# Page slots that rotate, and pooling tables that are loaded earlier, in a one-core decoder step

## The reference

```
Layer 0 mixer, samples (mla_sample): for each of the 8 sequences
    rows   = cache[16 pages] (2048 x 320), and the new row
    kn     = rmsnorm(latent @ w_uk) per head;  s = (qn.kn + qr.kr) * scale
    p      = softmax(s);  ctx = p @ latent;  o = ctx @ w_uv
Layer 1 mixer (pool_mixer): per group of 256 channels
    d      = mean over the last 2/4/8/16 positions - the position itself
    y      = (d @ w_pool[group]) * pool_scale
Both layers (peer): q = x @ w_q; s = q @ subkeys; two top-16, top-16 of their sums
    e      = 128 experts per token;  g = softmax(best)
    y      = sum_k g_k * gelu(x . u[e_k]) * v[e_k]
Every sub-layer: rmsnorm, (1 + scale) * h + shift from c, gated residual add
```

## Time and profile before

| | |
|---|---|
| Time of the runs | 3461.2 us (3457.77 to 3462.1) |
| Span of the profiled execution | 3450.9 us, from first to last instruction |
| Time beside the span | 10.3 us (3461.2 - 3450.9) |
| PE, DVE, ACT, POOL busy | 80%, 66%, 30%, 35% of the span |
| Moved from HBM | 1258.79 MB |
| Chain that ended last | PE 44%, DMA 27%, DVE 15% |

### The profile page before, as it was taken

The page is one execution under the profiler, slowest core; times in us unless marked ns, Lnnn a source line. Parts: engine busy times, 40 slices in busy tenths (PEclk is TensorE's granted clock), DMA queues, the critical chain, the costliest instruction groups (busy, mean ns, idle before and its releaser), DMA issues.

```text
span 3450.9 us, 39502 instructions
## 1 busy us (share of the span) xinstructions
PE 2764.3 (80%) x11255; PEld 1233.7 (36%) x11255; DVE 2273.6 (66%) x6378; ACT 1043.5 (30%) x4438; POOL 1212.1 (35%) x1077
## 2 busy tenths in 40 slices
PE   7889889879989858988989779889875675566765
PEld 2355544434434323434433234334331231112321
DVE  2544668887787856768777566777866545565455
ACT  1222324424434413434434314434411111111111
POOL 0000024333333424434434334433344444543343
PEclk9989999989999979999999989999888876777777
DMA  8740079999999989999999999999999999999998
GB/s 326 285 176 34 14 275 406 401 374 397 366 395 407 396 332 401 413 390 417 413 401 412 396 357 412 415 404 410 395 396 414 418 421 408 421 389 376 421 417 356
DMA packets 201396, 1264.74 MB, mean 366 GB/s; under 512 B 23689, under 2 KB 44730, under 8 KB 61393
## 3 DMA queue, kind: packets, MB, share of 16 engines
q0 software_dynamic: 150784, 1091.03, 77.5%
q1 hardware_dynamic: 50393, 171.18, 12.9%
HBM read 1258.79 MB, written 3.79 MB: 366 GB/s over the span
## 4 chain that ended last, share of the span: by engine, by line
PE 44%; DMA 27%; DVE 15%; issue 7%; ACT 3%; POOL 2%; SPq 2%; DVEq 0%; POOLq 0%; ACTq 0%; PEldq 0%
PE bank L1146 15%; DMA ring<-in_uv,work 10%; PE bank L884 7%; DMA mod_mix<-in_uv,work 7%; DMA big<-in_uv,work 6%; PE bank L996 6%; DVE ring L2028 2%; PE bank L901 2%; DMA ring<-in_w_ada 2%; PE bank L830 2%; ACT work L1475 1%; PE bank L698 1%; PE bank L728 1%; PE bank L636 1%; PE bank L872 1%
## 5 line engine op out<-in xcount | busy, mean ns | idle before, releaser
L1146 PE MATMUL bank<-ring,work 128*64 128x512 f32 (+1 forms) x2080 | 903.6, 709 | 272.3 <-ACT work L1475 272.2
L1514 POOL DMA_INDIRECT ring<-in_uv,work x520 | 602.8, 1159 | 937.9 <-PE bank L1146 810.0
L2028 DVE CUSTOM_DVE_ANT_0 ring<-ring,mod_smp 128x1024 f32<-128x1024 f32 x512 | 621.8, 1224 | 264.7 <-DMA ring<-in_uv,work 257.7
L1463 ACT ACTIVATE work<-work 128x2 f32<-128x2 f32 x520 | 105.1, 202 | 1485.7 <-DVE work L2028 1485.2
L1514 POOL DMA_INDIRECT big<-in_uv,work x260 | 305.1, 1174 | 663.3 <-PE bank L1146 361.2
L884 PE MATMUL bank<-big 128*128 128x512 f32 x1024 | 515.2, 626 | 0.0
L1146 PEld LDWEIGHTS bank<-ring,work 128*64 128x64 f32 (+1 forms) x2080 | 209.3, 153 | 623.5 <-ACT work L1475 386.2
L1146 PE MATMUL bank<-big,work 128*64 128x512 f32 (+1 forms) x1040 | 308.0, 710 | 153.1 <-ACT work L1475 153.1
L2028 DVE CUSTOM_DVE_ANT_0 big<-big,mod_smp 128x1024 f32<-128x1024 f32 x256 | 309.5, 1224 | 133.4 <-DMA big<-in_uv,work 129.7
L1146 PE MATMUL bank<-work 128*64 128x512 f32 (+1 forms) x520 | 295.6, 697 | 106.2 <-ACT work L1475 106.1
L1475 ACT ACTIVATE work<-small,work 128x64 f32<-128x64 f32 (+1 forms) x1040 | 303.2, 339 | 144.7 <-DVE work L2038 138.8
(11 more groups left out here) (301 smaller groups left out, 3419.2 us busy)
## 6 DMA issues: line engine op xcount, KB each, us to landing
big<-in_wk SPq DMA_DIRECT2D x48, 1152.0 KB, 10.5
ring<-in_w_ada SPq DMA_DIRECT2D x64, 768.0 KB
work<-in_cache_mla SPq DMA_DIRECT2D x104, 160.0 KB, 6.5
ring<-in_uv,work POOLq DMA_INDIRECT x520, 12.0
big<-in_uv,work POOLq DMA_INDIRECT x260, 11.3
ring<-in_w_mla_out SPq DMA_DIRECT2D x1, 4096.0 KB, 14.0
big<-in_w_mla_out SPq DMA_DIRECT2D x4, 1024.0 KB, 11.5
mod_smp<-in_cache_mla SPq DMA_DIRECT2D x24, 160.0 KB, 11.1
```

Of the source, the lines that this page charges most:

```text
L1146: last = mm(out, diag[:, t % 2, j, 0:min(m, HALF)], s[:, D + half * 512:D + (half + 1) * 512], start=(k == 0 and (n < S0 or j == 0)), stop ...
L1463: act.activation(acts[:, t % 2 * GRP:(t % 2 + 1) * GRP], dots[:, t % 2 * GRP:(t % 2 + 1) * GRP], ACT.Gelu)\
L1514: pool.indirect_dma_start(slot[g % SLOTS], None, T["uv"].rearrange("l e d -> (l e) d"), bass.IndirectOffsetOnAxis(index[:, k * GRP + j:k * ...
L2028: dve.tensor_tensor_reduce(u, u, hb, 1.0, 0.0, ALU.mult, ALU.add, dots[:, at:at + 1]).then_inc(sem("dots_set"), 1)
```

## The change

Sample pages get 25 slots instead of 16. Page g of sequence r lies in slot (16 r + g) mod 25, nine of which are in a new buffer `pages_ahead` of 12 KB to a partition; the scratch for POOL's transfer descriptors is set to 4096 bytes to a partition. SP loads the next sequence's first 9 pages at `tail - 8` and its other 7 and the own row at `tail + 5`. Its first page is computed at `tail + 2` instead of `tail + 7`; `project_page` now waits for the step of the softmax before it whose part of PSUM bank 6 it writes, and `spread_max` writes to columns 256 to 383 instead of 0 to 127. The last sequence's `tail` is turn 314 instead of 345; `out_turn`, 360, and the number of turns stay as they were.

For the pooling mixer, two modulation rows, `norm_mix`, band and w_pool are loaded at turn -11. `norm_mix` goes to a free `hid` buffer. The third row and `pool_scale` are loaded at turn -1.

```diff
-        PGRP = 4
+        PGRP, EARLY = 4, 9
+        pages_ahead = sb("pages_ahead", [P, 3 * D])
...
-        cached = [cached_all[:, g * ROW:(g + 1) * ROW] for g in range(13)]
-        cached += [mod_smp[:, 2, g * ROW:(g + 1) * ROW] for g in range(3)]
+        page_slots = [cached_all[:, g * ROW:(g + 1) * ROW] for g in range(13)]
+        page_slots += [mod_smp[:, 2, g * ROW:(g + 1) * ROW] for g in range(3)]
+        page_slots += [pages_ahead[:, g * ROW:(g + 1) * ROW] for g in range(EARLY)]
+        cached = lambda r, g: page_slots[(r * NPG + g) % len(page_slots)]
...
             tail[r_] = t_
-            t_ += 7
+            t_ += 2
...
-                    if t == tail[r - 1] + 4:
+                    if t == tail[r - 1] - 8:
+                        if r >= 2:
+                            sp.wait_ge(sem("ctx_ps"), r - 1)
+                        sp.wait_ge(sem("page_ps"), (r - 1) * NPG + EARLY)
+                        load_pages(r, 0, EARLY)
+                    if t == tail[r - 1] + 5:
                         sp.wait_ge(sem("ctx_ps"), r)
-                        load_pages(r)
+                        load_pages(r, EARLY, NPG)
...
-                    if t == mix_at[n] - 2:
+                    if t == mix_at[n] - 11:
+                        sp.wait_ge(sem("qT_ps"), n // 2 * PH)
+                        for m, k in ((0, 1), (1, 0)):
+                            ld(mod_pool[:, m, :], ada_rows[1, NC - 1, k * D:(k + 1) * D].partition_broadcast(P), "mods_in")
+                        ld(hid[n % 4], T["norm_mix"][1].partition_broadcast(P), "mods_in")
+                        sp.wait_ge(sem("sco_ps"), n // 2 * PH)
+                        pooling_weights()
+                    if t == mix_at[n] - 1:
                         sp.wait_ge(sem("choice_set"), n // 2 * 2 * PH)
-                        mods(mod_pool, 1, 0, "prompt", P, T["norm_mix"][1], gain_pool)
+                        ld(mod_pool[:, 2, :], ada_rows[1, NC - 1, 2 * D:3 * D].partition_broadcast(P), "pool_gain_in")
+                        ld(gain_pool, T["pool_scale"][0].partition_broadcast(P), "pool_gain_in")
                     if t == mix_at[n] + 2:
                         w.next("mods_set")
-                        ld(gain_pool, T["pool_scale"][0].partition_broadcast(P), "pool_gain_in")
...
-                for n in mix_at:
-                    if t == mix_at[n] - 2:
-                        sp.wait_ge(sem("sco_ps"), n // 2 * PH)
-                        pooling_weights()
...
-                if g == 0 and r:
-                    pe.wait_ge(sem("ctx_ready"), r)
+                if r:
+                    gone = page_at[r, g] - tail[r - 1]
+                    if gone >= 7:
+                        pe.wait_ge(sem("ctx_ready"), r)
+                    elif gone >= 5:
+                        pe.wait_ge(sem("ctx_norm"), r)
+                    elif gone >= 3:
+                        pe.wait_ge(sem("s_shift"), r)
+                    else:
+                        pe.wait_ge(sem("max_diag"), r)
...
-                        set_mods(mod_pool, P, gain_pool)
+                        set_mods(mod_pool, P, hid[n % 4], ("mods_in", 16, 3))
...
-    nc = bacc.Bacc("TRN2", target_bir_lowering=False, num_devices=1)
+    nc = bacc.Bacc("TRN2", target_bir_lowering=False, num_devices=1, dynamic_dma_scratch_size=4096)
```

More of the change, by code:

```diff
@@ L491, in _, with load_pages @@
             sp.wait_ge(sem("first_set"), 1)
-            def load_pages(r):
-                for g in range(NPG):
+            def load_pages(r, first, end):
+                for g in range(first, end):
                     page = sp.value_load(pages[0:1, r * NPG + g:r * NPG + g + 1], min_val=0, max_val=T["cache_mla"].shape[1] - 1)
-                    ld(cached[g], T["cache_mla"][0, bass.ds(page, 1)].rearrange("a p n -> (a p) n"), f"page_in{g // PGRP}")
-                ld(cached_own[0:1, :], O["rows_s"][0, r:r + 1, 0, 0:KL], f"page_in{NPG // PGRP}")
+                    ld(cached(r, g), T["cache_mla"][0, bass.ds(page, 1)].rearrange("a p n -> (a p) n"), f"page_in{g // PGRP}")
+                if end == NPG:
+                    ld(cached_own[0:1, :], O["rows_s"][0, r:r + 1, 0, 0:KL], f"page_in{NPG // PGRP}")
             def pooling_weights():
@@ L545, in turn @@
                     w.next("table_in", 16)
-                    load_pages(0)
+                    load_pages(0, 0, NPG)
                     ld(O["pst_s"][0, :, 0:STATE - 1, :], T["state_pool"][0, :, 1:STATE, :], "state_out")
@@ L861, in turn_page @@
                 for c in range(KLC):
-                    pe.transpose(pb[7][:, c * P:(c + 1) * P], cached[g][:, c * P:(c + 1) * P], ident)
-                pe.transpose(pb[7][0:ROPE, 2 * P:3 * P], cached[g][:, KL:ROW], ident).then_inc(sem("page_ps"), 1)
+                    pe.transpose(pb[7][:, c * P:(c + 1) * P], cached(r, g)[:, c * P:(c + 1) * P], ident)
+                pe.transpose(pb[7][0:ROPE, 2 * P:3 * P], cached(r, g)[:, KL:ROW], ident).then_inc(sem("page_ps"), 1)
             def project_page(r, g):
@@ L889, in spread_max @@
                 pe.wait_ge(sem("s_max"), r + 1)
-                pe.transpose(pb[6][0:NH, 0:P], tiny[:, 8:8 + NH], ident).then_inc(sem("max_ps"), 1)
+                pe.transpose(pb[6][0:NH, 2 * P:3 * P], tiny[:, 8:8 + NH], ident).then_inc(sem("max_ps"), 1)
             def spread_max2(r):
@@ L900, in context @@
                 for g in range(NPG + 1):
-                    last = mm(pb[6][0:NH, 160:160 + KL], ps_s[:, g, :], cached[g][:, 0:KL] if g < NPG else cached_own, start=(g == 0), stop=(g == NPG))
+                    last = mm(pb[6][0:NH, 160:160 + KL], ps_s[:, g, :], cached(r, g)[:, 0:KL] if g < NPG else cached_own, start=(g == 0), stop=(g == NPG))
                 last.then_inc(sem("ctx_ps"), 1)
@@ L1876, in top @@
                 dve.wait_ge(sem("max_ps"), r + 1)
-                dve.tensor_reduce(tiny[0:NH, 34:35], pb[6][0:NH, 0:P], AX_X, ALU.max).then_inc(sem("smp_tail"), 1)
+                dve.tensor_reduce(tiny[0:NH, 34:35], pb[6][0:NH, 2 * P:3 * P], AX_X, ALU.max).then_inc(sem("smp_tail"), 1)
                 dve.wait_ge(sem("smp_tail"), r * 2 + 1)
@@ L1956, in background @@
                     if t == mix_at[n] + 1:
-                        set_mods(mod_pool, P, gain_pool)
+                        set_mods(mod_pool, P, hid[n % 4], ("mods_in", 16, 3))
                     if t == mix_at[n] + 5:
-                        w.next("pool_gain_in", 16)
+                        w.next("pool_gain_in", 16, 2)
                         d(tt(mod_pool[:, 2, :], mod_pool[:, 2, :], gain_pool, ALU.mult))
```

## The result

The changed kernel takes 3479.3 us (median of 8 runs, 3466.8 to 3491.8); the kernel before took 3459.0 us beside it on the same chip (8 runs, 3452.3 to 3465.6). The ratio is 1.0065, 95% interval 1.005 to 1.0081: slower by about 20 us, where 25 us faster were forecast. The forecast's direction was wrong and the time lies 19 us above the range.

The account below looks back on a forecast made before the run. Transfers were taken to bound late turns, transfers and PE almost equally page turns. Mixer loads -23, pages -2 and scratch 0 gave -25 us: span 3450.9 to 3426, median 3436 us; range for 8 in 10: 3408 to 3460.

Parts of the forecast that it names:

- Part A: Earlier loads for the two pooling mixers win back idle DMA time: -23 us, bounds -38 and -4.
- Part C: The smaller descriptor scratch for POOL's gathers was taken to cost 0 us, bounds 0 and +10.
- Part B: Sample pages at two turns between sequences instead of seven: -2 us, bounds -33 and +47.
- Two turns of the gap still have no page: Between sequences, two page-free turns save about 2.4 us of PE each, 4.8 us taken off each gap's cost.
- PE's waits for late pages are gone: PE's waits for late pages, 14.8 us in the whole span, vanish: 2.1 us for each gap.
- The price of a cycle: Page stage, sequence to sequence: 39 turns before at 220.4 us, 34 turns now at 227.1 with 5 moved to the end.
- a cycle over 197: Sign against the forecast in the page stage: a cycle of 34 turns taking over 197 us.
- PE above 90% in the gaps: Sign for the forecast: between sequences PE stays above 90% busy.
- Two: Rival: page turns are at PE's limit, context and softmax waits exposed; Part B +47, 3485 us; chance 0.09.
- one: Rival: the mixers' transfer is hidden anyway; Part A at its small end, Part B 0, 3457 us; chance 0.13.
- three: Rival: more than the sum, gaps lose their dips too and mixers gain fully; 3407 us; chance 0.13.
- four: Rival: mixer loads late again, pages ahead landing 15 us later; about 10 us of Part A lost, 3446 us; chance 0.07.

Follow-up runs that it names:

- e2: The kernel before with only the mixers' loads moved (turn -11, the third row and pool_scale at -1): 3429.5 us, ratio 0.9915.
- e3: The kernel before with the descriptor scratch at 4096 bytes and nothing else: 3460.8 us, ratio 1.0002.
- e1: The changed kernel with seven turns between sequences again instead of two, all else kept: 3434.3 us, ratio 0.9936.
- e5: The changed kernel with no page at tail +4 and +5, the turns at the context: 3446.8 us, ratio 0.9965.
- e13: The changed kernel with no page at tail +12 and +13, where no context or softmax step stands: 3478.1 us, ratio 1.0046.
- e7: The kernel before with the mixers' loads moved and the context's products split over two turns, seven-turn gaps and old page loads: 3448.6 us, ratio 0.9974.
- e4: The changed kernel whose context adds up only 2 of its 17 products: 3435.9 us, ratio 0.9935.

## Why the prediction was wrong

**What bounds the kernel** was read rightly as far as it went: transfers late, transfers and PE together in page turns, the mixers as the two large holes.

**Part A**, -23 us with bounds -38 and -4, was right: e2 measured -30, a little more than the idle time counted behind the waits. The reckoning of the loads held as well. Seven pages and the set were to land in 64 us; w_pool landed 54.5 us after the first of these pages was issued (1174.8 to 1229.3), and bytes shared evenly would have made it 23. The landing is much nearer to the 64 and so agrees with what the Trainium skill (DMA: Bandwidth & Descriptors, section Queues, rings and completion order) says of engines that go round between queues packet by packet. The forecast of 370 GB/s around the mixers failed, 362 and 348. With the pages as before it holds: in e2 the first stretch has 390:

```profile
1248.00:1328.00 80.00, 57.39 (x230) 27.09 (x227) 62.31 (x136) 16.44 (x65) 29.64 (x26) 0.80 0.96 390
```

**Part C**, 0, was right: e3's ratio is 1.0002.

**Part B** is the term that was mis-sized: -2 us taken, +45 for the gap measured by e1 (+50 for all the page work, changed kernel against e2). The bound named in the text, +47 "if nothing is absorbed", is what happened. The working had the cost in hand: 6.7 us for a gap by the context's products and the softmax waits in page turns; the tail table has 6.4 for an end (55.0 - 48.6), and eight of these are 51, of which some 10 come back elsewhere (the turns 0 to 519 together differ by 41). Two steps then took it away, and a third hid it.

- *"Two turns of the gap still have no page and save about 2.4 us of PE each."* These are +0 and +1, and the context stands at +4. They took 13.6 us together in the changed kernel (14.6 before), not less than two page turns of 5.56. Free turns help the context only close to it: e5 got 32 us for two of them, e13 nothing that shows. I subtracted PE time as if it could be kept for later, and it can be only as far as the slots reach.
- *"PE's waits for late pages are gone, 2.1 us for each gap."* They did go, 14.8 us to 3.0, but were worth nothing that shows: e1 has 3.5 us of them and is not faster than e2, which has 13.6. Waits of this size inside free turns show no cost; those of e7, 48.5 us, did cost time.
- The price of a cycle hid this. The two cycles of 39 turns in the trace of before took 217.7 and 215.2 us, not 220.4: the eight turns behind `tail` took 47.7 and 47.5, as reckoned, but the others 5.45 each, not 5.56. The changed kernel's three cycles of 34 turns took 194.8, 197.4 and 189.6, mean 193.9, just what the forecast makes of 34 turns (220.4 - 0.2 - 26.3 = 193.9). That agreement is luck. The turns outside the eight take 5.42 there, so 34 turns were priced 4.8 us too high; and of the 11.8 us of context and softmax waits 9.7 stayed, where the forecast left 4.9. The sign to look for, a cycle over 197, was too lax for the same reason: it came true in one of the three.

By these cycles a gap costs 3.8 us more (193.9 + 26.3 - 216.4), 26 for seven, and not the 45 that e1 measured. They cannot settle more. In e3 and e1 the two cycles of 39 turns took 220.1 and 216.9, and 223.4 and 216.2, so one cycle is known to a few us only, and most gaps lie in cycles that cross a mixer or a tile's end, which the forecast did not price apart. A slip of little weight: 35 turns were to come free behind turn 314, but 345 - 314 is 31, as the turns barred to pages fall differently.

PE above 90% in the gaps, which I named as a sign of success, says nothing good: over the eight turns of the fifth end PE is busy 84% (48.14 of 57.10 us), and in the 20 us where it is at 100% the DMA share is 0.73.

**The rivals.** Two, slower at PE's limit, 3485 us and given 0.09, came true with almost its own numbers; its mechanism, context in page turns, is what e1, e4 and e5 show. What I held against it, that PE waited as much in the gaps before, mistook slack for waste: those idle microseconds were what took up the context's 7.8 us. As an estimate: in the late turns PE is busy 53 of 100 us, so a free turn of 5.3 leaves some 2.5 us, and a context needs about three of them. Of the softmax part of that rival, +2 and DVE's 4.62 us, the runs show only that the turn and the wait are longer. Rivals one and three need a Part B near zero or better and fall with it; four needs w_pool late, and it was 24 us early.

**The new waits in `project_page`**, given nothing, do not show among PE's waits in the changed kernel. What showed was the opposite direction: DVE and the expert turns waiting for PE.

## What to carry to other kernels

An engine's idle time beside a bound transfer can be what absorbs short heavy steps there; before filling it with work from elsewhere, add up all that the engine then has to do in the few turns that the buffers cover, not only its longest piece, and compare it with the time of those turns. Idle time near the heavy step counted here, and idle time elsewhere brought nothing that showed. A mean busy share over a stage tells none of this. When a change has several parts, price both sides of each difference from the same kind of rows, cycle against cycle, and run the parts apart: here one was worth -30 us and another +45.

## What was not expected of the hardware

Nothing of the chip itself went against the forecast. Two numbers are worth keeping: a quarter of the descriptor scratch made no difference to a queue that moves 1091 MB (ratio 1.0002 [0.9988, 1.0015]), and the slots gave only a few turns of cover: at the fifth end, amid full page turns, 13.9 us of other work on PE went with a 13.45 us wait on POOL and a DMA share of 0.73 for 20 us, where plain page turns have 1.00.
